# Half of a weight piece sent ahead, norm rows on row groups, and two bias sums moved behind the convolution in a one-core decoder block

## What is computed

```python
mod = silu(c) @ w_ada + b_ada                       # 6 x 1024: shift1, scale1, gate1, shift2, scale2, gate2
h = rms_norm(x, norm1_g) * (1 + scale1) + shift1
p = h @ w_in                                        # conv a | conv gate | q | k | v | f | gate_c | gate_a
u = conv_a * sigmoid(conv_gate)
u = causal_depthwise_conv(u, w_dw, width 31) + b_dw
y_conv = silu(group_norm(u, 8 groups of 64)) @ w_conv_out
q, k = rms_norm(q), rms_norm(k)                     # per head of 64, 8 heads each
s = q k^T / 8 + cumsum(log_sigmoid(f)) differences, causal; y_attn = (softmax(s) v) @ w_attn_out
x = x + gate1 * ((sigmoid(gate_c) * y_conv + sigmoid(gate_a) * y_attn) @ w_out)
h = rms_norm(x, norm2_g) * (1 + scale2) + shift2
x = x + gate2 * (top-8-of-64 experts(h) + shared_expert(h))
```

## Time and profile before

| | us |
|---|---|
| median of 3 runs (lowest, highest) | 725.06 (723.65, 725.34) |
| the profiled execution | 724.96 |
| its span in the trace | 723.2 |
| PE busy | 665.1 |
| DVE busy | 305.8 |
| ACT busy | 172.1 |
| POOL busy | 33.7 |

### The profile page before, as it was taken

One profiled execution on the slowest core, in us unless ns is written; L12 is line 12 of the kernel. 1 busy time (PEld: TensorE's weight loads), 2 busy tenths in 40 slices (PEclk: granted clock), 3 DMA queues, 4 the chain that ended last, 5 costly groups with the idle time before them and its releaser, 6 DMA issues.

```text
span 723.2 us, 10076 instructions
## 1 busy us (share of the span) xinstructions
PE 665.1 (92%) x3371; PEld 375.2 (52%) x3371; DVE 305.8 (42%) x690; ACT 172.1 (24%) x307; POOL 33.7 (5%) x61
## 2 busy tenths in 40 slices
PE   2899999999999999999998989989989989998896
PEld 0478866888886487664433423434334433443333
DVE  2338989988243477442232223122321222222224
ACT  2010133213220241222322312123221321232211
POOL 7001112000000001000000000000000000000001
PEclk9999999999999999999999999989999999999999
DMA  8999989633420006428999999999999999999961
GB/s 302 387 387 322 390 304 344 239 127 127 177 87 0 1 3 261 205 80 328 407 428 427 428 423 425 429 429 425 423 425 430 424 427 425 429 426 424 425 276 58
DMA packets 43132, 225.65 MB, mean 312 GB/s; under 512 B 3488, under 2 KB 3520, under 8 KB 29414
## 3 DMA queue, kind: packets, MB, share of 16 engines
q1 hardware_dynamic: 41528, 224.43, 76.9%
q10 hardware_dynamic: 1582, 0.94, 0.5%
HBM read 224.31 MB, written 1.05 MB: 312 GB/s over the span
## 4 chain that ended last, share of the span: by engine, by line
PE 58%; DMA 34%; SPq 3%; DVE 3%; issue 1%; ACT 0%; DVEq 0%
DMA raw<-n_w_experts_gate_up_dram 31%; PE bank L1166 16%; PE bank L1502 14%; PE bank L1450 4%; PE bank L1305 4%; PE bank L1337 4%; DMA ring<-in_w_in_dram 3%; PE bank L1486 3%; PE bank L1194 2%; SPq L320 2%; PE bank L1492 1%; PE bank L1460 1%; SPq L324 1%; PE bank L1510 1%; PE bank L1117 1%
## 5 line engine op out<-in xcount | busy, mean ns | idle before, releaser
L1502 PE MATMUL bank<-raw,hT 128*32 128x512 f32 x832 | 102.6, 650 | 27.1 <-DMA raw<-n_w_experts_gate_up_dram 27.1
L1166 PE MATMUL bank<-work,ring 128*128 128x256 f32 x512 | 116.1, 384 | 1.7 <-DMA ring<-in_w_in_dram 1.7
L1166 PEld LDWEIGHTS bank<-work,ring 128*128 128x128 f32 x512 | 97.2, 192 | 17.3 <-issue 2.9
L1486 PE MATMUL bank<-raw,hT 128*128 128x512 f32 x224 | 99.9, 599 | 0.3 <-DVE ST L1045 0.3
L1065 DVE TENSOR_TENSOR sg<-sg,bank 128x256 f32<-128x256 f32 x27 | 11.4, 421 | 177.8 <-ACT sg L651 177.8
L1502 PEld LDWEIGHTS bank<-raw,hT 128*32 128x32 f32 x832 | 31.9, 118 | 96.7 <-issue 96.7
L1486 PEld LDWEIGHTS bank<-raw,hT 128*128 128x128 f32 x224 | 41.4, 190 | 58.9 <-issue 58.1
L1460 PE MATMUL bank<-y,ST 128*128 128x512 f32 x224 | 70.5, 436 | 0.5 <-DVE y L1074 0.5
L651 ACT ACTIVATE sg<-bank 128x256 f32<-128x256 f32 x27 | 17.1, 635 | 211.1 <-PE bank L1502 120.9
L1050 DVE TENSOR_SCALAR SI<-iota,slotm,wt 128x32 f32 (+2 forms) x108 | 30.1, 315 | 56.6 <-issue 56.6
L1460 PEld LDWEIGHTS bank<-y,ST 128*128 128x128 f32 x224 | 39.0, 189 | 24.1 <-issue 17.6
(11 more groups left out here) (279 smaller groups left out, 584.5 us busy)
## 6 DMA issues: line engine op xcount, KB each, us to landing
raw<-n_w_experts_gate_up_dram SPq DMA_DIRECT2D x53, 2048.0 KB, 16.7
raw<-in_w_experts_down_dram SPq DMA_DIRECT2D x53, 1024.0 KB, 18.4
ring<-in_w_ada_dram SPq DMA_DIRECT2D x12, 2048.0 KB, 18.5
ring<-in_w_in_dram SPq DMA_DIRECT2D x9, 2048.0 KB, 13.2
ring<-in_w_out_dram SPq DMA_DIRECT2D x2, 2048.0 KB, 8.5
ring<-in_w_attn_out_dram SPq DMA_DIRECT2D x1, 2048.0 KB, 19.0
ring<-in_w_conv_out_dram SPq DMA_DIRECT2D x1, 2048.0 KB, 7.6
ring<-in_w_shared_gate_up_dram SPq DMA_DIRECT2D x1, 2048.0 KB, 7.8
```

The lines of the kernel that those rows point to most:

```text
L1166: ins = mm(b[:, kk * SEQ:(kk + 1) * SEQ], w[:, k, m * PART:(m + 1) * PART], h1T[:, k, :], start=(k == 0), stop=(k == KD - 1))
L1486: ins = mm(psU[:, :], hT[:, k, :], wg[:, k, :], start=(k == 0), stop=(k == KD - 1))
L1502: ins = mm(psU[c:c + 32, :], hT[:, k, c:c + 32], w_gu(s)[:, k, :], start=(k == 0), stop=(k == KD - 1))
```

## The change

First, the first half (blocks 0 to 3) of the first `in` piece is issued behind the second mod piece, and its second half where the piece stood. Units 0 and 1 write four banks instead of two, and PE computes their blocks 0 to 3 between the mod pieces. Second, the pieces `ada` 6 and 7 go to the end of the list, and their sums, bias additions, matmuls and copies move: DVE sums the first ahead of the merge and the second behind it, PE's matmuls stand ahead of the output projection and in its middle. POOL's iota, which waits for the last of them, moves along. Third, the `headrow` matmuls contract over 32 partitions each, in two rounds, with a wait of PE on itself between the rounds.

```diff
-                 ("in", 2), ("ada", 3), ("in", 3), ("ada", 4), ("ada", 5), ("in", 4), ("ada", 6), ("ada", 7),
-                 ("in", 5), ("in", 6), ("in", 7), ("in", 8)]
+                 ("in", 2), ("ada", 3), ("in", 3), ("ada", 4), ("ada", 5), ("in", 4),
+                 ("in", 5), ("in", 6), ("in", 7), ("in", 8), ("ada", 6), ("ada", 7)]
...
+        EARLY_B = [(1, 5), (2, 6)]
...
-        ADA2_B = [7, 0, 7, 0, 7, 0, 7, 5]
+        ADA2_B = [7, 0, 7, 0, 7, 0, 7, 7]
...
-                sp.dma_start(piece(n), pieces[n]).then_inc(piece_in[n % NBUF], 16)
+                if n == EARLY:
+                    sp.dma_start(piece(n)[:, KD // 2:KD, :], pieces[n][:, KD // 2:KD, :]).then_inc(piece_in[n % NBUF], 16)
+                else:
+                    sp.dma_start(piece(n), pieces[n]).then_inc(piece_in[n % NBUF], 16)
+                if n == MOD[1]:
+
+                    sp.dma_start(piece(EARLY)[:, 0:KD // 2, :], pieces[EARLY][:, 0:KD // 2, :]).then_inc(early_in, 16)
...
-                    ins = a.activation(gsig[:, 2 * u:2 * u + 2, :], ps2, ACT.Sigmoid)
+                    for kk in range(2):
+                        ins = a.activation(gsig[:, 2 * u + kk, :], bank[EARLY_B[u][kk]][:, 0:SEQ], ACT.Sigmoid)
...
+            ada_out(6)
+            ada_out(7)
 
             def exp_z(t):
...
             mod_row_out(0)
+            mod_column(0)
             mod_row_out(1)
-            mod_column(0)
-            mod_row_out(2)
             mod_column(1)
             h1_out(1)
+            mod_row_out(2)
+            mod_column(2)
             mod_row_out(3)
-            mod_column(2)
             mod_column(3)
             h1_out(3)
...
             taps(2)
-            ada_sum(10)
 
             v.wait_ge(qkstat, 1)
             v.tensor_scalar(rs16[:, :], bank[6][:, 0:SEQ], EPS, None, ALU.add).then_inc(qkstat, 1)
-            ada_sum(11)
             v.wait_ge(qkrstd, 1)
...
+            ada_sum(10)
             for i in range(4):
                 v.wait_ge(yc_done, i + 1)
...
-            v.wait_ge(ada2_out, 8)
+            v.wait_ge(ada2_out, 6)
             v.wait_ge(n2_in, 16)
             link(v.tensor_tensor(G2, G2, n2g, ALU.mult))
+            ada_sum(11)
...
                 if t == 1:
                     clip(0)
+                else:
+                    v.wait_ge(ada_done, 8)
...
+            mod_columns(0)
+            mod_piece(1)
+            mod_columns(1)
+
+            pe.wait_ge(early_in, 16)
+            pe.wait_ge(h1T_act, 2)
+            pe.wait_ge(h1T_dve, 2)
+            project_in(0, (0, 1), range(0, 4))
+            mod_piece(2)
+            project_in(1, (0,), range(0, 4))
+            mod_columns(2)
+            mod_piece(3)
+            project_in(1, (1,), range(0, 2))
             mod_columns(3)
+            project_in(1, (1,), range(2, 4))
...
-                    project_in(u, (0, 1))
+                    project_in(u, (0, 1), range(KD // 2, KD) if u < 2 else range(KD))
...
-            for i in range(4):
-                for kk in range(2):
-                    ins = mm(bank[UNIT_B[i % 4]][:, kk * SEQ:(kk + 1) * SEQ], headrow[:, 2 * i + kk, :], rs16[:, :],
+            for rnd in ((0, 3, 5, 6), (1, 2, 4, 7)):
+                for k in rnd:
+                    g = slice(32 * (k % 4), 32 * (k % 4) + 32)
+                    ins = mm(bank[UNIT_B[k // 2]][:, (k % 2) * SEQ:(k % 2 + 1) * SEQ], headrow[g, k, :], rs16[g, :],
                              start=True, stop=True)
-                ins.then_inc(qkb_done, 1)
+                    if rnd[0] == 1:
+                        ins.then_inc(qkb_done, 1)
+                if rnd[0] == 0:
+                    ins.then_inc(qkb_half, 1)
+                    pe.wait_ge(qkb_half, 1)
...
-            for i in range(2):
-                for kk in range(2):
-                    ins = mm(bank[1 + i][:, kk * SEQ:(kk + 1) * SEQ], headrow[:, 2 * i + kk, :], rs16[:, :], start=True, stop=True)
-                ins.then_inc(cb_done, 1)
+            for k in (0, 2, 1, 3):
+                g = slice(32 * k, 32 * k + 32)
+                ins = mm(bank[1 + k // 2][:, (k % 2) * SEQ:(k % 2 + 1) * SEQ], headrow[g, k, :], rs16[g, :], start=True, stop=True)
+                if k == 2:
+                    ins.then_inc(cb_half, 1)
+                    pe.wait_ge(cb_half, 1)
+                if k % 2 == 1:
+                    ins.then_inc(cb_done, 1)
...
+            ada(10)
 
             pe.wait_ge(merged, 4)
...
+                    if (t, n) == (1, 0):
+                        pe.wait_ge(ada2_out, 7)
+                        ada(11)
```

More of the change, by code:

```diff
@@ L208, in hybrid_conformer_fox_moe_block @@
         (AOUT, COUT, WOUT, SHGU, SHD) = (21, 22, 23, 25, 26)
+        EARLY = order.index(("in", 0))
         MOD = [order.index(("mod", j)) for j in range(4)]
@@ L1151, in _, with project_in @@
                 ins.then_inc(h1T_ps, 1)
[L1152 to L1154 removed]
+            def project_in(u, halves, ks=range(KD)):
+                w = piece(UNIT_PIECE[u])
+                for kk in halves:
+                    m = 2 * (u % 2) + kk
+                    b = bank[EARLY_B[u][kk] if u < 2 else UNIT_B[u % 4] if u < 10 else M_B[u % 2]]
+                    at = 0 if u < 2 else kk * SEQ
+                    for k in ks:
+                        ins = mm(b[:, at:at + SEQ], w[:, k, m * PART:(m + 1) * PART],
+                                 h1T[:, k, :], start=(k == 0), stop=(k == KD - 1))
+                if kk == 1 and KD - 1 in ks:
+                    ins.then_inc(unit_done, 1)
+            mod_columns(0)
[10 more added lines that the diff above has]
+            project_in(1, (1,), range(0, 2))
             mod_columns(3)
+            project_in(1, (1,), range(2, 4))
             pe.wait_ge(h1T_act, 4)
             pe.wait_ge(h1T_dve, 4)
[L1159 to L1169 removed]
             def forget_and_stats():
@@ L1266, in _ @@
             pe.wait_ge(ada2_out, 6)
-            pe.wait_ge(ada2_out, 7)
             scores(0)
@@ L1341, in h2_turned @@
             def h2_turned(t):
+                if t == 1:
+                    pe.wait_ge(ada2_out, 8)
                 for i in range(2):
```

29 lines of the change are left out of this document (7 added, 22 removed).

## The result

| | before | changed |
|---|---|---|
| median (lowest, highest) of 4 runs each | 725.20 (723.65, 726.21) | 719.29 (717.72, 720.22) |
| ratio, 95% interval | | 0.9918, 0.9891 to 0.9945 |
| profiled execution, its span | 724.96, 723.2 | 720.09, 718.3 |
| PE busy | 665.1 | 656.6 |

The forecast was 719.9 us. The two profiled executions differ by 4.87 us, the medians by 5.9.

A forecast was written before the change was run, and what follows sets the result against it. PE work ahead of the experts was taken as the bound, each microsecond won there reaching the end. 724.96 less 2.8 (halves), 0.9 (ada matmul), 2.1 and 0.2 (rows), plus 0.9 (output projection) gave 719.9 us, range 718.0 to 722.4.

The forecast's parts named there:

- rival E: Last expert pass: it falls on the full clock, 1.6 us less, 718.3 us; chance 0.1.
- Edit 1: Kernel start: early half of the first projection piece; PE's first ada matmul at 51.05 instead of 53.83, gain 2.8 us.
- the sum: Whole kernel: 724.96 - 2.8 - 0.9 - 2.1 - 0.2 + 0.9 = 719.9 us.
- The bound from below (2.1): Kernel start: if the clock stays low once more for 3 us, units end at 51.7 and 2.1 us gain remain.
- Rival D: 28 to 43 us: early matmuls delay the mod pieces at half clock, units 11 us late, 733.8 us; chance 0.03.
- rival C: Fifth sum (0.3 us slack) or third projection piece (1.5 us) comes late, PE waits up to 1 us, 720.9; chance 0.12.
- Edit 2: Second gate's two sums moved: 0.9 us gained before the norm rows, 0.9 us paid in the output projection.
- Edit 3: Norm rows by row groups: 1.5 us at each place, gaining 2.1 us at the first and 0.2 at the second.
- The upper bound on the gain, 4.0 us: Norm rows: with no overhead in the rounds, a gain of 4.0 us.
- Rival A: Norm rows: row groups do not overlap, a round takes 1.5 us, 2.2 us given back, 722.1 us; chance 0.11.
- Rival B: PE's stop before the first ada matmul, about 50 us, halves the clock and loses 1.6 us, 721.5; chance 0.13.

The follow-up runs named there:

- second execution: The changed kernel profiled again with nothing altered; this execution took 718.75 us.
- the halves alone: The kernel before with only the early half of the first projection piece and its first 16 matmuls between the mod pieces; median 721.21 us, ratio 0.9948.
- third execution: The changed kernel profiled once more with nothing altered; this execution took 718.62 us.
- the later sets: The changed kernel timed again in two further sets of runs; medians 718.42 and 718.49 us, ratios 0.9916 and 0.9900 to the kernel before.
- the rows alone: The kernel before with only the norm-row matmuls on row groups in two rounds; median 724.04 us, ratio 0.9989.
- the iota held back: The kernel before with the norm rows on row groups, and POOL's iota delayed until the merge is done; one execution, 724.46 us.
- the rounds of two: The changed kernel with the q/k norm rows in four rounds of two matmuls instead of two rounds of four; one run, 719.77 us.
- the reordered ring: The changed kernel with the second and third projection pieces ahead of ada pieces and every ada matmul one unit later; medians 715.62 and 718.40 us.

## Why the prediction was right, point by point

**What bounds the kernel.** Right: a microsecond won on PE ahead of the experts reached the end. 4.56 us at the first pass became 4.87 in the time of the profiled execution. Behind that pass the stretch is the same but for tenths and for one thing, rival E: from that pass to the end of the span it takes 400.6 us in the first profile of the changed kernel, whose last trio pass ran at half clock, and 399.2 and 399.0 in the other two, where it took 7.07 us.

**Edit 1.** Right in mechanism and place: PE's ada matmul at 50.87 for 51.05, POOL as releaser, 2.8 us. In this execution the walk up to it was off by 1.9 us. The early matmuls began 0.6 us sooner than in the sum and ran at full clock where it had put 5 us, so the units ended at 48.1 instead of 50.0 and the wait was 2.76 instead of 1; the gain did not feel it, since POOL's end is what counts. The second execution is the one that the sum describes: 5.38 us for the early matmuls, the units over at 49.8, a wait of 1.10. The bound from below (2.1) was reached as well: with the halves alone and 6.74 us for the early matmuls the ada matmul stood at 51.54, 2.1 before 53.67. A fall that cost 2.9 us in the third execution left 2.58, since the wait pays for most of it.

What the sum did not see is that before's 53.67 was one draw. Five executions with before's start and nothing added to it (two of before, three with later edits alone) stand at 53.67, 54.70, 54.46, 54.98 and 55.94, mean 54.75; five with the early halves and the ada matmul behind unit 1 at 50.87, 50.91, 51.09, 51.54 and 50.79, mean 51.04. That is 3.7 us, 0.9 more than between the first two profiles, and the halves alone gained 3.8 us in the timed runs (2.5 to 4.9). It is the likeliest reason why the medians moved by 5.9 us, and by 6.2 and 6.8 in the later sets, where the profiles moved by 4.9: over the same five and five, 3.71 at the start, 1.76 from there to the expert loop (268.56 to 266.80) and 0.36 behind it give 5.8. Rival D, "the early matmuls delay the mod pieces at half clock", came true in a small part in two of three executions: the third mod piece started 1.7 and 2.9 us later than in the first, but ran at full clock itself (1.92 us), and the clock was back long before the units ended. That was harmless for the reason that the sum gives, the slack at POOL.

**The suppliers behind it (rival C).** The slack of 0.3 us at the fifth sum was 0.14, and it cost tenths. POOL's step ran from 87.53 for 1.44 us, to 88.97, just as PE reached its matmul (89.11), and in the chain the pair took 1.10 us instead of 0.86: 0.24 lost, which I put down to the late signal, though no wait is recorded. The other executions fit: the pair took 1.03 to 1.10 us in three more where PE came 0.15 to 0.21 us behind POOL's end, and 0.86 with the halves alone, where it came 0.6 us behind. With the first pair, which started from a standstill, the shift is 2.45 us at the first v unit instead of 2.8. The third piece was in time.

**Edit 2.** Right: PE's start of the norm rows moved by ACT's copy alone (115.27, behind a wait of 0.78), 0.86 more than the shift ahead of it. The ada matmul in the merge's gap cost nothing, the one in the output projection 0.86; the second half of w_out was issued at 212.9 and nothing waited for it. What the working missed is on DVE: it noted that the iota's stretch goes, and put no price on it. With edit 3 and the iota in its old place it would have cost 0.8 us (the kernel with the rows alone against the one with the iota held back), because the rows by then come early enough for DVE to be the later one.

**Edit 3.** Right in kind and, within a tenth, in size: 1.44 us for 1.5. The parts don't fall out as the sum has them: two rounds at 0.6 with 0.3 between them were forecast, and the chain shows rounds of 0.75 and 0.71 with 0.04 between them. Whatever the first weight load of a round costs lies inside the round. The total holds because the two misses cancel. The upper bound on the gain, 4.0 us, is more than its own terms give: 3.61 + 1.73 - 4 x 0.43 = 3.6. The group norm took 1.40 for 1.5 (1.72 before). Rival A, 1.5 us for a round of four, is refuted by the 0.72, and the rounds of two confirm it. The four row groups made four matmuls 2.5 times as fast (4 x 0.45 = 1.80 against 0.72); the 3.07 times of the Trainium skill's "TensorE: Matmul & The Clock Gate", "Measured speedup vs the span model", is for 512 columns, and for these 256 columns of float32 it was too high. By it a round would be 0.6, an estimate; the measured 0.72 decides.

**Rival B.** A stop of 2.76 us, more than the 1 us in question, was followed by full clock (1.00 on both sides of it). In three executions of the changed kernel the clock fell at about 28 or not at all, and never behind this stop; but only one of the three had a long one, the others 1.10 us and none.

**The sum.** At the first pass of the expert loop 4.56 us for the 5.1 forecast. The missing 0.5 us are 0.35 ahead of the v units (the slow pair, the late fifth sum), 0.1 at the norm rows (1.99 between their start and the scores for 2.1) and 0.1 at the group norm, whose shift at the output projection is 0.12 for 0.2. The profiled execution, 720.09, is 0.2 over the forecast, and the median, 719.29, is 0.6 under it. What brings the median down is rival E, to which the prediction gave 0.1: in the second and third execution the expert loop starts where it did in the first (317.73 and 317.77 against 317.67), but the last trio pass runs at full clock, and they took 718.75 and 718.62. So part of the nearness to 719.9 is luck. The sum promised 0.5 us too much on PE and assumed, with before's profile, a last pass at half clock, which only one of the three executions had. In before's own profile two draws cancel, the earliest start of the five and a slow last pass (401.0 us from the first pass to the end of the span, 398.8 in its second execution), which is why its 724.96 lies close to the median.

## What to carry to other kernels

A wait for a supplier whose time is fixed (here DMA, DVE and POOL) is also a buffer: work moved in front of it may run slower, by as much as the wait is long, without moving what follows. The kernel's spread seems to shrink with it. Before a term is summed against one profile, ask whether its start is the same in another execution; a second profile of the unchanged kernel had this start 1.03 us later. An edit that is worth nothing alone can hold the cover of another, so test the parts together as well as one by one.

## What the runs showed of the hardware that was not expected

- The clock's fall is tied to the execution, not only to the stop. The same program, with the same wait of 1.42 us just before, had its early matmuls at full clock once (27.80:31.00, PEclk 1.00), at 0.63 once and at 0.50 once.

```profile
27.80:31.00 3.20, 3.20 (x10) 2.56 (x10) 0.00 (x0) 0.00 (x0) 0.00 (x0) 0.63 1.05 387
```

```profile
27.80:31.00 3.20, 3.20 (x8) 2.57 (x9) 0.00 (x0) 0.00 (x0) 0.00 (x0) 0.50 1.05 387
```

  (the first stands in the section on the profile after; here come the second and the third).
- PE can be slow where PEclk says 1.00: the first mod piece takes 3.64 us in the changed kernel and the second 1.92, and the transposes of the reordered ring took 3.46 us instead of 1.86, each in a stretch with PEclk 1.00. The reason stays open.
- A round of float32 matmuls over row groups with 256 columns costs 0.70 to 0.75 us, with two or with four groups in it, and a wait of PE for its own result adds 0.04 us to the chain.
